# Delta layer: the copies of k, q and QK on GpSimd, moved from behind the chain of substitutions to its column 18

## What is computed

```python
kk = jnp.einsum('bhik,bhjk->bhij', kc, kc)
m = jnp.where(strict, bc[..., :, None] * kk * decay, 0.0)
rhs = jnp.concatenate([vc * bc[..., None], kc * (bc * jnp.exp(G))[..., None]], axis=-1)
sol = lax.linalg.triangular_solve(m + eye, rhs, left_side=True, lower=True, unit_diagonal=True)
u, w = sol[..., :DV], sol[..., DV:]
v_new = u - jnp.einsum('bhck,bhkv->bhcv', w, S)
qk = jnp.einsum('bhik,bhjk->bhij', qc, kc) * decay
o = einsum(qc * exp(G), S) + einsum(qk, v_new)
S = S * exp(g_last) + einsum(kc * exp(g_last - G), v_new)
```

## Time and profile before

| what | value |
|---|---|
| median of three runs | 3915.2 us (3910.34 to 3916.56) |
| time of the profiled execution | 3931.21 us |
| its span, first to last instruction | 3929.4 us |
| mean granted TensorE clock | 0.937 |
| busy: PE, DVE, ACT, POOL | 92%, 59%, 34%, 23% |

### The profile page before, as it was taken

The page is one execution under the profiler, slowest core; times in us unless marked ns, Lnnn a source line. Parts: engine busy times, 40 slices in busy tenths (PEclk is TensorE's granted clock), DMA queues, the critical chain, the costliest instruction groups (busy, mean ns, idle before and its releaser), DMA issues. The chain is left out here.

```text
span 3929.4 us, 70243 instructions
## 1 busy us (share of the span) xinstructions
PE 3615.9 (92%) x25857; PEld 3443.6 (88%) x25857; DVE 2325.8 (59%) x3903; ACT 1342.9 (34%) x2859; POOL 915.9 (23%) x1114
## 2 busy tenths in 40 slices
PE   5889999999999989999779999699999999999799
PEld 3878889988888988888769999499999999999799
DVE  4567778777777777777643222456656656566422
ACT  3333333433433443333322111233333433333322
POOL 0344555444555444455500000000000000000000
PEclk8989999999999999999889999899999999999899
DMA  3322332222333223233125333333333333232343
GB/s 110 99 64 74 83 89 71 73 74 76 82 81 83 77 64 81 76 82 86 43 81 152 101 105 97 93 98 97 88 91 91 88 98 96 82 95 78 110 131 94
DMA packets 624335, 346.96 MB, mean 88 GB/s; under 512 B 93811, under 2 KB 592358, under 8 KB 623686
## 3 DMA queue, kind: packets, MB, share of 16 engines
q1 hardware_dynamic: 532086, 273.70, 25.8%
q10 hardware_dynamic: 92160, 72.05, 6.3%
HBM read 296.54 MB, written 49.13 MB: 88 GB/s over the span
## 5 line engine op out<-in xcount | busy, mean ns | idle before, releaser
L823 PE MATMUL main<-xh,w_hi 128*128 128x280 f32 x3072 | 724.8, 318 | 38.6 <-DVE w_lo L1047 38.6
L823 PE MATMUL main<-xl,w_hi 128*128 128x280 f32 x3072 | 654.1, 295 | 0.0
L823 PE MATMUL main<-xh,w_lo 128*128 128x280 f32 x3072 | 653.8, 294 | 0.0
L823 PEld LDWEIGHTS main<-xh,w_hi 128*128 128x128 f32 x3072 | 501.8, 194 | 55.3 <-issue 45.6
L823 PEld LDWEIGHTS main<-xh,w_lo 128*128 128x128 f32 x3072 | 497.8, 192 | 0.0
L823 PEld LDWEIGHTS main<-xl,w_hi 128*128 128x128 f32 x3072 | 497.1, 192 | 0.0
L1780 PE MATMUL b_main<-xh_b,b_w_hi 128*128 128x280 f32 x2048 | 477.0, 315 | 12.4 <-DVE b_w_lo L1985 12.4
L1780 PE MATMUL b_main<-xh_b,b_w_lo 128*128 128x280 f32 x2048 | 438.4, 296 | 0.0
L1780 PE MATMUL b_main<-xl_b,b_w_hi 128*128 128x280 f32 x2048 | 436.8, 295 | 0.0
L779 POOL TENSOR_TENSOR Tl<-Tl,prod 40x30 f32<-40x30 f32 (+14 forms) x480 | 354.4, 738 | 37.6
L1780 PEld LDWEIGHTS b_main<-xh_b,b_w_hi 128*128 128x128 f32 x2048 | 332.1, 193 | 23.9 <-issue 12.5
(11 more groups left out here) (275 smaller groups left out, 6356.8 us busy)
## 6 DMA issues: line engine op xcount, KB each, us to landing
w_raw<-in_a_w_in SPq DMA_DIRECT2D x192, 512.0 KB, 4.0
a_w_raw<-in_a_w_out SPq DMA_DIRECT2D x64, 512.0 KB, 4.1
b_w_raw<-in_kv_w SPq DMA_DIRECT2D x64, 512.0 KB, 4.1
b_w_raw<-in_b_w_in SPq DMA_DIRECT2D x64, 512.0 KB, 4.1
y_w_raw<-in_b_w_out SPq DMA_DIRECT2D x32, 512.0 KB, 5.4
o<-ot ACTq DMA_DIRECT2D x16, 560.0 KB, 3.2
a_o_raw<-o SPq DMA_DIRECT2D x32, 280.0 KB, 3.9
b_kc<-in_cache_k ACTq DMA_DIRECT2D x16, 512.0 KB, 4.9
```

What stands on the lines that cost most here:

```text
L823: m = nc.tensor.matmul(main[2 * (t % 2) + h][:, 0:HALF], hi[:, n % SPLIT_RING, k, :], x[:, KSUB * (n % 2) + k, h * HALF:(h + 1) * HALF], s ...
```

## The change

The four copies become a function `swap(turn)`, which the chain calls when it comes to column j = 18, ahead of that column's product. The waits are the same but for the one on the chain's end, which is left out. The step `swap` of the written order stays as a place without work. Nothing else is changed: the copies, their semaphore counts, the order of the other engines.

```diff
+SWAP_AT = 18
...
+            def swap(turn):
+
+                wait(pool, kq_made.after(turn))
+                wait(pool, kkq_took.after(turn, 2))
+                wait(pool, ks_sum.after(turn, SAMP))
+                wait(pool, os_sum.after(turn, SAMP))
+                same(kqk[:, :, 0:2, :], kq[:, :, 1:3, :], slice(0, P)).then_inc(swapped.sem, 1)
+                same(kqk[:, :, 2, :], kq[:, :, 0, :], slice(0, P)).then_inc(swapped.sem, 1)
+                for h in range(2):
+                    r = slice(C * h, C * h + C)
+                    wait(pool, swapped.after(turn, n=2 + h))
+                    same(QK[r, :, C - C * h:P - C * h], QKc[r], r).then_inc(swapped.sem, 1)
...
                         for j in range(1, SUB - 1):
+                            if j == SWAP_AT:
+                                swap(turn)
...
-                    elif what == "swap":
-                        wait(pool, kq_made.after(turn))
-                        wait(pool, kkq_took.after(turn, 2))
-                        wait(pool, ks_sum.after(turn, SAMP))
-                        wait(pool, os_sum.after(turn, SAMP))
-                        wait(pool, chained.after(turn))
...
```

## The result

| what | before | after |
|---|---|---|
| median of four runs each | 3912.77 us (3895.18 to 3916.56) | 4049.4 us (4040.58 to 4052.84) |
| ratio of the two | | 1.0355, 95% interval 1.0319 to 1.0391 |
| span of the profiled execution | 3929.4 us | 4048.2 us |
| granted TensorE clock | 0.937 | 0.929 |

The change makes the kernel 3.6% slower. The forecast was 4049 us.

A forecast was written before the change was run, and what follows sets the result against it. The prediction took a closed ring of inv5a, TensorE work, GpSimd's chain and T's way through DRAM as the bound. Copies 131.2, DVE 4 and the removed wait -1 gave +134 us, 4049 us; range for all 4015 to 4090.

The forecast's parts named there:

- The ring: Turn's closed cycle: inv5a, 52.8 us of TensorE work and transfers, 53.05 us of chain, 10.2 us of T, inv5a.
- The copies in the chain, 131.2 us: Four copies moved into GpSimd's chain: 127.2 us busy plus 4.0 of gaps, 8.2 us a turn, all added.
- GpSimd beside DVE, 4 us: Column 18 onward: mutual hold-up's sum taken as the same, plus 0.3 us a turn for heavier DVE work, 4 us.
- The rest of the ring: From inv5a to the next chain: 52.8 us of TensorE work and transfers, with no change allowed for.
- The clock, 0 us: TensorE's low-clock stretch after inv5a, now 13.6 us, changes by -2.2 to +1.7 us; nothing taken.
- The wait at column 18, nothing: Copies' wait for the scan's last block, which ends 6.6 us earlier; margin moves along, cost nothing.
- TensorE's stall of about 15 us: TensorE's stop at inv5a for T grows from some 6 us to some 15 in each turn.
- The sum: Whole kernel: 131.2 + 4 - 1 = +134 us, 4049 us against the median, 3.4% slower.
- That the copies held the turn: Rival at TensorE's seq1 wait for QK: its 101.3 us come back, 3814 us; chance 0.03.
- Relief from DVE: Rival on GpSimd: copies fall to 6.2 us, later columns to 16.8, so +43 us, 3959 us; chance 0.06.
- The late scan: Rival at column 18: the 6.6 us margin is gone, by 4 us a turn, 56 more, 4105 us; chance 0.07.
- That something else hides the move: Rival: the move does nothing because SyncE or TensorE waits for something else; chance 0.02.

The follow-up runs named there:

- experiment 1: Kernel before with the four copies shrunk to one or two elements a partition, at their old place behind the chain: 3919.24 us, ratio 1.0005.
- experiment 3: Changed kernel with the copies at column 18 replaced by four fills of kqk, each with a tiny copy behind it: 4067.1 us, ratio 1.0383.
- experiment 4: Changed kernel with the four copies done twice at column 18: 4157.97 us, ratio 1.0600 against the kernel before.
- experiment 8: Kernel before with T's loads issued from two queues, inv5a ahead of seq1, and Tl stored and loaded earlier: 3859.19 us, ratio 0.9859.
- experiment 2: Changed kernel with the copies at column 18 shrunk to one or two elements a partition, all waits kept: 3948.95 us, ratio 1.0081.

## Why the prediction was right

**The ring.** It held. `inv5a` follows the chain's end by 10.0 to 10.8 us in every turn of both kernels; the copies' time came onto the chain, and experiments 1, 3 and 4 show it from three sides: taking the copies away behind the chain gives nothing back, other work at column 18 costs its length too, and a second set of copies costs 109 us more.

**The copies in the chain, 131.2 us.** A size was off here. The prediction took their length from the place behind the chain, 8.3 us a turn. At column 18 they take 6.2 to 7.1: 106.1 us busy and 2.5 of gaps, 108.6 in all, 22.6 less.

**GpSimd beside DVE, 4 us.** Off the other way, by 15.7 us. The direction was right (copies beside lighter work, columns beside heavier), the size was not: the columns grew by 674.6 - 654.9 = 19.7 us. The step on "the sum as the same" is what held: 108.6 + 19.7 = 128.3, against 131.2 + 4.

**The rest of the ring.** Nothing was allowed for it, and it gave a little back. The last `inv5a`, before and after:

```profile
1965.82 1.46 PE L865 MATMUL E<-T1s,W 128*128 128x32 f32 x6 [20.43 <-DMA TT<-T]
```
```profile
2078.79 3.60 PE L869 MATMUL E<-T1s,W 128*128 128x32 f32 x16 [22.46 <-DMA TT<-T]
```

The delta layer's last `inv5a` came 113.0 us later, where 134 were forecast. The copies and columns make 128.3. Added up over 15 turns, the stretches from `inv5a` to the next chain came to 785.5 us in place of 792.2, 6.7 less. The chain's first two instructions (lines 766 and 769, now 780 and 783) took 59.2 us in all in place of 65.1, 5.9 less. The rest is under 3 us.

**The clock, 0 us.** The low stretch counted from `inv5a` was put at -2.2 to +1.7 us against 13.6. Two windows of the changed kernel behind `inv5a`, the first at the low level throughout, the second at the full one:

```profile
1221.30:1233.60 12.30, 12.28 (x51) 11.56 (x51) 1.22 (x1) 4.98 (x10) 0.00 (x0) 0.50 0.47 126
1234.00:1240.00 6.00, 6.00 (x48) 5.95 (x47) 4.49 (x5) 0.85 (x2) 0.00 (x0) 1.00 0.00 0
```

So at this boundary a longer stall did not mean a longer low stretch behind it. The low level ended 12.3 to 12.7 us behind `inv5a`, 0.9 to 1.3 us sooner than before. At half speed that is 0.45 to 0.65 us, about what the next chain came sooner behind `inv5a` here (52.2 us in place of 52.8).

**The wait at column 18, nothing.** Right: no gap ahead of the copies, 0.0 us in all turns. The margin was 4.3 us here and not 6.6, so it did not quite move with the ring.

**TensorE's stall of about 15 us.** Too long: 10.96 us here. TensorE came later to `inv5a`, partly through the waits for `on` (line 913, 43.8 us, 18 times), where DVE is held up beside the copies. By the ring that delay costs nothing, since the stall behind it is shorter by as much; in experiment 3, where that wait is missing, the stall was 12 to 16 us in all turns but the first and the last.

**The sum.** 134 us against 4049.4 - 3912.8 = 136.6 us between the medians, but 4048.2 - 3929.4 = 118.8 us between the two profiled executions. The agreement to a fraction of a us is in part luck. By the traces the sum was 15 us too high, and 21 against the 113.0 us of the delta layer alone. The profiled execution of before was one of its longer ones: its 15 runs beside the experiments spread from 3893.64 to 3934.21 us, with a granted clock of 0.943 in the fastest and 0.937 in the slowest. And from the last `inv5a` to the end, where most of the work is code that no version touches, the ten traces took from 1959 to 1983 us. What makes single executions of that kernel differ by 1% stays open.

**The rivals.** That the copies held the turn is refuted by experiment 1, and by 8, where `inv5a` starts ahead of the copies' end and the kernel is faster. Relief from DVE came for the copies and was paid back by the columns. The late scan costs when the copies stand at column 9, not at 18. That something else hides the move is out with the result.

## What to carry to other kernels

When one event releases two paths and the list of waits names the shorter of them because it stands first in the engine's order, removing that wait only hands it to the next line; lay the timelines beside each other and see which path ends last. Work that ran beside a transfer was free here, and moving it ahead of the event that starts the transfer made it cost its length in every turn. The gain lay in the path that TensorE's list of waits put third, with 28.6 us: two queues for ten small loads and an earlier store took 1.4% off.

## What was not expected of the hardware

A two-input w_lo on DVE took 4.29 us beside the copies and 1.22 beside fills of the same tile on GpSimd. This fits the rule of the Trainium skill (SBUF — State Buffer, Who interferes with whom) that such an instruction contends with a GpSimd instruction that reads SBUF and not with one that only writes it. The w_lo ended at 1181.87 + 4.29 = 1186.16, 1.1 us behind the two kqk copies (1181.54 + 3.52 = 1185.06). So its length fits, to 0.1 us, a wait through both of them and then a run of its usual 1.2 us. Copies of one or two elements still cost GpSimd 0.9 to 1.9 us for four of them in experiment 2.
